# Retention layer of a two-layer model: three blocks of instructions made into one, with heads, norm and output product interleaved into the projection chunks

## What is computed

```python
proj = h @ w_in                                   # 1024 -> 6144
q, k, v, g = jnp.split(proj, [D_MODEL, 2 * D_MODEL, 4 * D_MODEL], axis=-1)
q = rotary(q, cos, sin); k = rotary(k, cos, sin)
# per head, chunks of 128 tokens
qk = jnp.einsum('bhnd,bhmd->bhnm', qc, kc) * dmask
inner = jnp.einsum('bhnm,bhme->bhne', qk, vc)
...
o = ((o - mu) * lax.rsqrt(var + LN_EPS)).reshape(B, S, 2 * D_MODEL) * gn_g.astype(f32)
return (jax.nn.silu(g) * o.astype(h.dtype)) @ w_out
```

## Time and profile before

| | us |
|---|---|
| median of 3 runs | 2340.72 |
| the profiled execution's own time | 2337.77 |
| its span | 2336.1 |
| TensorE busy | 2111.5 (90%) |
| VectorE busy | 1574.5 (67%) |
| ScalarE busy | 1119.7 (48%) |
| GpSimd busy | 682.8 (29%) |

### The profile page before, as it was taken

The page is one execution under the profiler, slowest core; times in us unless marked ns, Lnnn a source line. Parts: engine busy times, 40 slices in busy tenths (PEclk is TensorE's granted clock), DMA queues, the critical chain, the costliest instruction groups (busy, mean ns, idle before and its releaser), DMA issues. The chain is left out here.

```text
span 2336.1 us, 34069 instructions
## 1 busy us (share of the span) xinstructions
PE 2111.5 (90%) x11356; PEld 1745.5 (75%) x11356; DVE 1574.5 (67%) x2566; ACT 1119.7 (48%) x1604; POOL 682.8 (29%) x466
## 2 busy tenths in 40 slices
PE   3988999997996689999968998998899998999997
PEld 3874777775875567777747554998899998888886
DVE  5356887886345648888859763199849997555554
ACT  3353677674341337766723032254444443545454
POOL 4720200002782530000011001489977774000000
PEclk7998999998998779999989999999999999999999
DMA  8864788894486238888931233154444443555554
GB/s 316 315 252 145 288 324 323 324 355 150 162 313 245 84 134 316 322 321 329 352 130 70 100 118 144 59 185 162 162 144 144 144 141 134 193 193 193 191 195 144
DMA packets 76319, 485.54 MB, mean 208 GB/s; under 512 B 9424, under 2 KB 9936, under 8 KB 58320
## 3 DMA queue, kind: packets, MB, share of 16 engines
q1 hardware_dynamic: 75520, 482.88, 56.9%
q10 hardware_dynamic: 720, 1.61, 0.2%
HBM read 483.41 MB, written 1.05 MB: 207 GB/s over the span
## 5 line engine op out<-in xcount | busy, mean ns | idle before, releaser
L1113 DVE TENSOR_TENSOR moe_w_lo<-ring,moe_w_hi 128x1024 fp32r<-128x1024 f32 x384 | 460.3, 1237 | 53.3 <-ACT moe_w_hi L1044 38.3
L1044 ACT ACTIVATE moe_w_hi<-ring 128x1024 fp32r<-128x1024 f32 x376 | 384.1, 1058 | 63.4 <-PE bank L993 35.9
L2806 POOL TENSOR_TENSOR peer_u_lo<-peer_u,peer_u_hi 128x512 fp32r<-128x512 f32 x256 | 347.5, 1369 | 115.6 <-ACT peer_u_hi L2829 114.6
L2769 PE MATMUL bank<-peer_hn_hi,peer_u_hi 128*128 128x256 f32 x1024 | 296.5, 290 | 19.5 <-POOL peer_u_lo L2806 19.5
L2770 PE MATMUL bank<-peer_hn_lo,peer_u_hi 128*128 128x256 f32 x1024 | 287.5, 281 | 0.0
L2771 PE MATMUL bank<-peer_hn_hi,peer_u_lo 128*128 128x256 f32 x1024 | 287.0, 280 | 0.0
L2829 ACT ACTIVATE peer_u_hi<-peer_u 128x512 fp32r<-128x512 f32 x256 | 161.0, 629 | 133.5 <-PE bank L2771 123.6
L225 POOL TENSOR_TENSOR ret_in_w_lo<-ring,ret_in_w_hi 128x1024 fp32r<-128x1024 f32 x48 | 117.7, 2466 | 348.6 <-ACT ret_in_w_hi L219 348.6
L974 PE MATMUL bank<-moe_w_hi,moe_slots_hi 128*128 128x512 f32 x512 | 209.2, 409 | 8.2 <-DVE moe_w_lo L1113 4.2
L2769 PEld LDWEIGHTS bank<-peer_hn_hi,peer_u_hi 128*128 128x128 f32 x1024 | 194.6, 190 | 22.8 <-POOL peer_u_lo L2806 21.5
L976 PE MATMUL bank<-moe_w_hi,moe_slots_lo 128*128 128x512 f32 x512 | 200.9, 392 | 0.0
(11 more groups left out here) (495 smaller groups left out, 4456.0 us busy)
## 6 DMA issues: line engine op xcount, KB each, us to landing
ring<-in_stream SPq DMA_DIRECT2D x135, 2048.0 KB, 7.9
peer_u<-in_peer_u SPq DMA_DIRECT2D x128, 512.0 KB, 3.3
peer_v<-in_peer_v SPq DMA_DIRECT2D x128, 512.0 KB, 3.3
sb_mod_ring<-in_ada_t SPq DMA_DIRECT2D x64, 512.0 KB, 9.0
ret_mod_ring<-in_ada_t SPq DMA_DIRECT2D x32, 512.0 KB, 8.5
s_bz<-in_b_channel SPq DMA_DIRECT2D x4, 512.0 KB, 5.9
ring<-in_stream SPq DMA_DIRECT2D x2, 1024.0 KB, 5.0
moe_room<-in_ln_g SPq DMA_DIRECT2D x3, 512.0 KB, 4.5
```

What stands on the lines that cost most here:

```text
L1044: act.activation(w_hi[:, q, :], K.ring[:, at % RING, q * CHUNK // Q:(q + 1) * CHUNK // Q], ACT.Copy).then_inc(hi_done, 1)
L1113: dve.tensor_tensor(w_lo[:, q, :], K.ring[:, at % RING, q * CHUNK // Q:(q + 1) * CHUNK // Q], w_hi[:, q, :].bitcast(F32), ALU.subtract).th ...
L2769: pe.matmul(out, u_hi[:, b, k2, :], h_hi[:, k, :], start=(k == 0), stop=False)
L2806: pool.tensor_tensor(u_lo[:, b, :, :], u[:, i, KD // 2 * half:KD // 2 * (half + 1), :], u_hi[:, b, :, :].bitcast(F32), ALU.subtract).then_ ...
```

## The change

The three blocks become one with 16 chunks in one `SplitProducts`, so that no engine waits for all others in between. Chunks 0 to 4 go as before. In chunks 5 to 8 two heads each are attended: scores, a quarter of the chunk's product, values (`scores`, `values`, `token_quarter`). PSUM banks 4 and 5 serve them, one each, where two each did before; the chunk products use banks 0 to 3. TensorE waits at chunk 5 until all rotations are done. VectorE subtracts the mean and multiplies by the norm's gain for the two heads at once (`centre`); the gain is no longer multiplied into the gate. In chunks 9 to 12, a chunk after its gate columns were made, two heads are multiplied by 1/std and gate (`open_pair`), turned after the chunk's third quarter (`turn_pair`) and split (`high_pair`, `low_pair`). Chunks 12 to 15 are the output product; each step of it waits for the `x_low` that it needs. The 32 folds stand three to a chunk in chunks 5 to 15, each fetched a chunk ahead. The normed rows `o` overlay the queries and keys of the head that is done, the layer norm's scratch overlays `o`, and the two rows of the layer norm go where the gain's row was.

The diff, cut to its core (the removed blocks stand whole in the listing above; line numbers in what follows are those of each kernel's own file):

```diff
+        FOLDS = {j: (3 * (j - FROM), min(3 * (j - FROM + 1), len(LATER_MODS))) for j in range(FROM, CH)}
+        s_b = scr[:, :, 0:W]
+        heads_of = lambda j: (2 * (j - FROM), 2 * (j - FROM) + 1) if FROM <= j < FROM + 4 else ()
+        pair_of = lambda j: j - 9 if 9 <= j < 13 else None
...
+        def banks_of(j):
+            return 2 * j % 6 if j < 4 else 2 * ((j + 1) % 2)
...
+                for j in range(CH):
+                    if j + 1 in FOLDS:
+                        mods.fetch(sp, *FOLDS[j + 1])
                     fetch_chunks(sp, K, n0 + j + 1 + RING)
-
-
+                    if j == 9:
+                        sp.wait_ge(centred, RET_HEADS)
+                        affine_rows(sp, K, 1, g_row, b_row, rows_in)
...
+                def scores(h):
+                    if h >= 1:
+                        pe.wait_ge(decayed, h)
...
+                def values(h):
+                    if h >= 1:
+                        pe.wait_ge(o_copied, h)
+                    pe.wait_ge(decayed, h + 1)
+                    pe.wait_ge(act_done, 5 + h // 2)
+                    pe.wait_ge(dve_done, 5 + h // 2)
...
+                def turn_pair(p):
+                    for h in (2 * p, 2 * p + 1):
+                        pe.wait_ge(out_ready, h + 1)
+                        if p:
+                            pe.wait_ge(x_low, h - 1)
+                        else:
+                            pe.wait_ge(o_copied, RET_HEADS)
...
+                for j in range(4, 12):
+                    evacuated = 2 if j == 4 else j - 1
+                    pe.wait_ge(act_done, evacuated)
+                    pe.wait_ge(dve_done, min(evacuated, 8))
+                    if j == FROM:
+                        pe.wait_ge(rotated, 8)
+                    for i, h in enumerate(heads_of(j)):
+                        scores(h)
+                        products.token_quarter(pe, n0 + j, i, [source(j, tt) for tt in range(TT)])
+                        values(h)
+                    for q in range(len(heads_of(j)), products.Q):
+                        products.token_quarter(pe, n0 + j, q, [source(j, tt) for tt in range(TT)])
+                        if q == 2 and pair_of(j) is not None:
+                            turn_pair(pair_of(j))
+                    products.retire(pe, n0 + j)
...
+                for j in range(12, CH):
+                    dh, part = divmod(j - 12, 2)
+                    if part == 0:
+                        pe.wait_ge(act_done, 11 + dh)
+                    for q in range(products.Q):
+                        if q % 2 == 0:
+                            pe.wait_ge(x_low, 4 * part + q + 2)
+                        products.token_quarter(pe, n0 + j, q, [K.bank[:, 2 * (1 - dh) + tt, :] for tt in range(TT)],
+                                               (x_hi, x_lo), part * KD, start=(part == 0), stop=(part == 1))
+                        if q == 2 and pair_of(j) is not None:
+                            turn_pair(pair_of(j))
+                        if q == 0 and j == 14:
+                            gate.tensor(pe)
+                    products.retire(pe, n0 + j)
+                    if part:
+                        pe.sem_inc(norm.y_made, TT)
...
+                for j in range(CH):
                     if j == FROM:
                         act.wait_ge(rotated, 8)
-                        act.activation(K.bank[:, 6:8, :].rearrange("p b c -> p (b c)"), K.c_row[:], ACT.Copy).then_inc(c_wide, 1)
-                    act.wait_ge(K.chunk_used, n0 + j + 1)
+                        act.activation(K.bank[:, 6:8, :].rearrange("p b c -> p (b c)"), K.c_row[:], ACT.Copy).then_inc(wide, 1)
+                    if j == 13:
+                        gate.scalar_diagonal(act)
+                    if j == 15:
+                        gate.scalar_take(act)
+                    for q in range(products.Q):
+                        if j + 1 < CH:
+                            products.high_quarter(act, n0 + j + 1, q, j + 1 < 4)
+                        if q < len(heads_of(j)):
+                            copy_values(heads_of(j)[q])
+                        if q == 2 and pair_of(j) is not None:
+                            high_pair(pair_of(j))
+                        if (j, q) in ((7, 2), (9, 1)):
+                            deviations((j - 7) // 2)
+                    if j < 12:
...
+                    for h in hs:
+                        for tt in range(TT):
+                            c.step(dve.bn_aggr(mv[:, h, tt, :], stats[:, h, tt, :]))
...
+                    if hs[1] % 4 == 3:
+                        dve.sem_inc(var_ready, 1)
+                    for h in hs:
+                        for tt in range(TT):
+                            c.step(dve.scalar_tensor_tensor(o[:, tt, h, :], o[:, tt, h, :], mv[:, h, tt, 0:1],
+                                                            rows[:, h * RET_V:(h + 1) * RET_V], ALU.subtract, ALU.mult))
+                    c.settle()
+                    dve.sem_inc(centred, 2)
+
+                def open_pair(p):
...
+                    if p % 2 == 0:
+                        dve.wait_ge(std_ready, p // 2 + 1)
+                        hs = slice(2 * p, 2 * p + 4)
+                        c.do(dve.reciprocal(std[:, hs, :], std[:, hs, :]))
+                    dve.wait_ge(act_done, 9 + p)
+                    for i, h in enumerate((2 * p, 2 * p + 1)):
+                        for tt in range(TT):
+                            c.step(dve.scalar_tensor_tensor(o[:, tt, h, :], o[:, tt, h, :], std[:, h, tt:tt + 1],
+                                                            opened[:, p % 2, tt, i * RET_V:(i + 1) * RET_V], ALU.mult, ALU.mult))
+                        c.settle()
+                        dve.sem_inc(out_ready, 1)
+
+                def low_pair(p):
+                    for h in (2 * p, 2 * p + 1):
+                        dve.wait_ge(x_high, h + 1)
+                        ks = slice(2 * h, 2 * h + 2)
+                        dve.tensor_tensor(x_lo[:, ks, :], K.bank[:, 4 + h % 2, :].rearrange("p (k t) -> p k t", k=2),
+                                          x_hi[:, ks, :].bitcast(F32), ALU.subtract).then_inc(x_low, 1)
...
+                for j in range(CH):
...
+                    folds = [(b, b + 1) for b in range(*FOLDS.get(j, (0, 0)))]
+                    if heads_of(j):
+                        first, second = heads_of(j)
+                        fade(first)
+                        mods.fold(dve, *folds[0])
+                        fade(second)
+                        moments(first)
+                        mods.fold(dve, *folds[1])
+                        moments(second)
+                        mods.fold(dve, *folds[2])
+                        centre((first, second))
+                    else:
+                        if pair_of(j) is not None:
+                            open_pair(pair_of(j))
+                        for b in folds:
+                            mods.fold(dve, *b)
+                        if pair_of(j) is not None:
+                            low_pair(pair_of(j))
+                    if j == 12:
+                        gate.vector(dve)
+                        norm.start(dve)
+                        dve.wait_ge(rows_in, 32)
+                    if j in (13, 14):
+                        affine(j - 13)
+                    if j < 8:
+                        dve.wait_ge(K.chunk_used, n0 + j + 1)
```

369 lines of the change are left out of this document (142 added, 227 removed).

## The result

The changed kernel takes **2297.18 us** (median of 4 runs, 2290.79 to 2297.75) where the kernel before, in the same comparison, takes 2339.39 (2333.44 to 2341.07): a ratio of 0.9826, 95% interval 0.9808 to 0.9844. Forecast were 2310.0 us, range 2302 to 2324.

The account below looks back on a forecast made before the run. TensorE was taken to bound the chunk products, VectorE and DMA the stretch between them. With 63.6 us taken away and 32.9 coming back, -30.7 against the median of 2340.72 gave 2310.0 us, range 2302 to 2324.

Parts of the forecast that it names:

- The gap of 63.6 us: Between chunk 11's last matmul and the output product, no chunk is multiplied; all 63.6 us were to go.
- the heads with their switches: Eight heads among TensorE's chunk products: 15.6 us, plus 2 us for about 40 changes of product.
- the transposes: All 32 turns on TensorE, at the full clock: 4 us back, ends 3.4 and 6.2.
- the wait for all rotations: TensorE starts chunk 5 only behind VectorE's last rotation: 5.1 us, hidden by nothing.
- the low clock behind it: Matmuls at half the clock after the idle at chunk 5: 2.5 us lost, ends 0 and 3.
- rival 3: Clock falls to 1.2 GHz in chunks 5 to 8, cut up by heads and turns: 2372 us, slower; chance 0.04.
- I take 1.5 for all four chunks: VectorE late with centring in chunks 5 to 8, so TensorE stalls: 1.5 us, ends 0 and 14.
- the openings: Chunks 9 to 12, multiplying heads by 1/std and gate: stall of 0.75 us a chunk, 3 in all.
- The ends 14 and 19: Upper ends for chunks 5 to 8 and 9 to 12, if every VectorE pass waits for a whole GpSimd subtraction.
- the pace carried over: A plain chunk was taken to cost TensorE 11.7 us, as in the kernel before.
- the cold quarter: Output product starts on a running TensorE, without its slow first quarter: 2.0 us lost before, 1.8 taken off.
- rival 1: Cover holds everywhere: no stalls, no loss of clock, free switches; -41.3 us, 2299.4 us; chance 0.10.

Follow-up runs that it names:

- busy_heads: Changed kernel with five 128 x 512 copies from PSUM on VectorE ahead of centring in chunks 5 to 8; 2317.13 us, ratio 0.9906.
- folds_as_before: Changed kernel with the 32 folds over chunks 5 to 11 again, four or five each; 2316.50 us, ratio 0.9906.
- swaps_early: Changed kernel with the last two swaps behind chunk 4's second quarter and VectorE rotating before it copies the chunk's values; 2291.42 us, ratio 0.9801.

## Why the prediction was wrong

**Right by its own steps.** The gap of 63.6 us goes, the heads with their switches cost 15.8 in chunks 5 to 8 (15.6 without), the transposes 3.6 (4), the wait for all rotations 5.2 (5.1), and the low clock behind it 2.4 (2.5). This last agreement is partly luck: in four variants with the same wait it cost 1.2 to 1.3. VectorE's passes lie in the forecast band. The clock held at 1.00 from 650 on in rows cut up by heads and turns, so rival 3 fell: the rule in the Trainium skill under "TensorE: Matmul & The Clock Gate", section "A second HAM failure mode: psum-queue depth-cycling", was not the outcome here, with at most 0.5 us of idle at a switch.

**Failed: "I take 1.5 for all four chunks" and "3" for the openings.** Measured 0. For the centring I had worked out a slack of about 1 us and then charged a stall all the same; busy_heads and folds_as_before show 1.1 and 1.16 us of it, and the changed kernel itself 1.21. For the opening I took "the second head is open at 8 to 10" us after the chunk's start, against 9.0: in chunk 9 it was done at 715.13, 7.5 us after 707.63, and 7.3 us after the start in chunks 11 and 12. My own terms gave no more: the Silu ready at 3.5 (as measured in chunk 9) or 2.2, and 4.5 for four passes, are 8.0 or 6.7, both before 9.0, so "8 to 10" and the charge did not follow from them. The ends 14 and 19 were not reached in any run, but what they stand for is real: a delay of 1 us is enough for 5.90 or 7.25 us in place of 4.

**Failed: the pace carried over.** "A chunk took TensorE (721.79 - 639.82) / 7 = 11.7 us" was used for a program whose buffers lie elsewhere. The pace is 11.45 there, 2.9 us over eleven chunks. No row of before told the two apart within retention, but the mixture's matmuls of the same form stepped at 0.2267 us in the same trace, and that should have told me that 0.2333 was no constant.

**Sizes.** Switches 0.4 for 2, tail 0 for 1 (VectorE had done the first halves of the layer norm before the last product ended), the transposes 3.6 for 4, the cold quarter 1.3 for 1.8, and 1.1, 0.7 and 0.4 us in chunk 0, the router and layer 0 that nothing in the change accounts for; the first two go with how long the granted clock was low there.

**The range** was too narrow downward. It took half of rival 1's stretch at 2299.4, and the large errors of the sum lay on one side. Stalls, switches and tail were charges that I had set above what they could come down to; the pace had no term and no bound at all. That the result lies nearest to rival 1 is in part luck: rival 1 had no loss of clock at chunk 5, and 2.4 us of it were paid. The pace (2.9), chunk 0 (1.1), the router (0.7) and the start (0.4), which stand in no case of the prediction, made up for it. Of the 2.2 us between 2299.4 and the measured median none is explained and none needs to be: between the two profiled executions the gain is 40.65 us, where rival 1 has 41.3. By the prediction's own signs, too, the result was too short rather than of another kind: 239.6 us from 567 to the mixture, with 240 as its lower limit, and chunks of 15.41, 12.36 and 11.47 us just under the bands that it gave.

## What to carry to other kernels

Where a slack has been worked out and is positive, charge nothing for the stall and put it into the range: cover is used up or it is not. But price the far side fully: here a wait of 2.5 us cost 2.8 to 4.4 us, because the clock went down with it, and a delay of 1 us on VectorE grew to 3 beside GpSimd. And take the pace of a row of matmuls as a property of the layout: when a change moves buffers, compare the steps first, and align wide operands if they differ.

## Not expected of the hardware

- The step of 128 x 512 matmuls depended on where their operands start in SBUF: 0.2267 us with the streamed weights at multiples of 256 bytes, 0.2289 at 64 more, 0.2322 to 0.2333 at 128 more. For the turned rows, as the loaded operand, 0.2267 at a multiple of 256 and 0.2333 at 224 more. The cause is open; loaded and streamed operand were each moved alone, but not in the same product.
- Behind a wait of 1.84 us (swaps_early) the clock was down, 0.57 in the next 4 us, and behind one of 2.55 us in chunk 7 of busy_heads it stayed at 1.00.
- The same wait of 4.6 to 4.7 us at chunk 5 cost 2.3 to 2.4 us of low clock in three kernels and 1.2 to 1.3 in four others.
- The same 32 products of the router took 3.9 to 4.5 us in six kernels and 6.98 in eight, and nothing in between was seen.
